# Where the activations of a feed-forward lie in SBUF, relative to the weights they meet

## The chip, the cores and the metric

One core of a Trainium2 chip runs the whole program in one launch. The metric is the device time of that core in microseconds. Three timed runs of the kernel before gave 2049.34 us in the median (2047.26 to 2052.21).

## The reference

Two blocks of layers, each of depth 2, on a sequence of 256 rows with 1024 columns in float32. The first block is a feed-forward, a mixer with sparse and block attention, and a second feed-forward:

```python
def swiglu(x, w_gate, w_up, w_down):
    return (jax.nn.silu(x @ w_gate) * (x @ w_up)) @ w_down

for l in range(DEPTH):
    x = x + 0.5 * swiglu(rms_norm(x, norm_ffn1[l]), ...)
    x = x + hybrid_mixer(rms_norm(x, norm_mix[l]), ...)
    x = x + 0.5 * swiglu(rms_norm(x, norm_ffn2[l]), ...)
```

The second block has a mixer with three branches (a recurrence, a retention and a spatial gate) and a feed-forward whose hidden columns go through a short convolution. A feed-forward widens 1024 columns to 2816 and comes back. There are six of them: four plain ones and two with convolution.

## The kernel before

Each float32 operand of a large product is held as two parts, a high one (rounded to the type float32r) and a low one (the rest). A product of two operands is three products on TensorE, `matmul3` (lines 82 to 90): high by high on line 88, high by low on line 89, low by high on line 90. In each the first operand (`lhs`) is loaded into the array as weights and the second (`rhs`) streams through it. A trace row names the moving operand first and the weights second.

A feed-forward (`ffn_phase`) runs over 11 chunks of 256 hidden columns. In a chunk, `hidden` makes the gate and up products: weights are 128 x 128 pieces of the gate and up matrices, the moving operand is the normed rows turned on their side, `hT`, 256 columns wide; that is 96 products. ScalarE and VectorE then form silu(gate) * up and split the outcome into a high and a low part in the tile `act`. In `down` the roles are turned: `act`, 128 x 128 at a time, is the weights, and the down matrix, 512 columns at a time, streams; that is 24 products a chunk. PE's order is hidden(i+1), down(i), hidden(i+2), down(i+1) and so on, so that a chunk's activations are ready long before they are used. Weights arrive by DMA in an `arrived` tile and are split by ScalarE (high, lines 384 and 394) and VectorE (low, lines 490 and 536) into `parts`.

Where the tiles lie is written out by hand, in columns of 4 bytes from a base. The plain feed-forwards use the map of the first block (`first_map`, base 45568), those with convolution the map of the second (`second_map`, base 58112). The start of a tile is base + 4 x column. Taken modulo 512 bytes:

| tile | plain feed-forwards | with convolution |
|---|---|---|
| `hT` (moving in gate and up) | 128 | 128 |
| gate and up parts (weights) | 448 | 448 |
| `act` (weights in down) | 128 | 128 |
| down parts (moving in down) | 448 | 448 |
| `arrived_down` (landing place) | 128 | 64 |

Other products of the same form lie elsewhere: the mixer's output product and its values job (`token_job`, projections by rows) have weights at 128 (`mixer_T_parts`) and a moving operand at 448 (`mixer_parts`); the second mixer's output product has weights at 320 (`merged_parts`) and a moving operand at 64 (`mix_parts`); its branch products have weights at 64 (`mix_parts`) and a moving operand at 64 (`branches_T`). Within these tiles the steps between slots, halves and parts are multiples of 512 bytes, but for the low part in the third slot of `mixer_parts`.

The distance between high and low part is 4096 bytes in `act` and `mix_parts`, 8192 in the down parts and in `merged_parts`.

Of the kernel before, what the change touches and what calls it, by code (L numbers as in the profile page):

```python
# [271 lines left out]
def blocks(first, *shape):  # L272

    width = KT * FF_W
    if not shape:
        return first
    step = width * int(np.prod(shape[1:]))
    return [blocks(first + n * step, *shape[1:]) for n in range(shape[0])]
# [526 lines left out]
def first_map(nc, c):  # L805

    def at(name, col, shape, dtype=F32):
        return nc.alloc_sbuf_tensor_at(name, shape, dtype, offset=FIRST_BASE + 4 * col)

    c.ffn = FfnMemory(at, "ffn", dict(hT=32, act=4128, arrived_down=6176, arrived=(blocks(9200, 2), blocks(23152, 2)),  # L810
                                      parts=(blocks(13296, 2, 2), blocks(27248, 2, 2)), down_parts=blocks(35440, 2, 2)))
    c.hT_parts = at("mixer_T_parts", 32, [P, 2, KT, S], F32R)
    c.wc1 = at("w_cmp1", 4128, [P, 2, CJ, CMP_HID])
    c.attention = at("attention", 4128, [P, 10 * S + N_WORK])
    c.branch_rows = at("branch_rows", 4128 + 10 * S + N_WORK, [P, 3, Q_COLS])
    c.wc2 = at("w_cmp2", 12320, [P, 2, 2, 2, DH])
    c.pos = at("pos", 43632 + W_UNIT, [P, 2, CJ])
    c.raw = at("raw", 12832, [P, N_TURNED, S])
    c.rot = at("rot", 17440, [P, N_ROT, S])
    c.vtok = at("v_tokens", 21024, [P, NT, 2 * P + Q_COLS])  # L820
    c.gates = at("gates", 22560, [P, NT, GATE_COLS])
    c.kc = at("k_cmp", 22608, [P, GROUPS, 16])
    c.vc = at("v_cmp_by_head", 22640, [P, NH, DH])
    widths = (UNIT, UNIT, W_UNIT)
    c.units_arrived = [at(f"mixer_arrived{n}", col, [P, w]) for n, (col, w) in enumerate(zip((23152, 25200, 43632), widths))]
    c.units_parts = [[at(f"mixer_parts{n}_{lo}", col + lo * w, [P, w], F32R)[:] for lo in range(2)] for n, (col, w) in enumerate(zip((27248, 31344, 35440), widths))]
    c.cos_part = c.work[:, 0:2 * S].rearrange("p (a n) -> p a n", a=2)

    c.kcols = c.h[:].rearrange("p t d -> p (t d)")[:, 0:2 * GROUPS * CJ * N_CMP].rearrange(
        "p (v g j n) -> p v g j n", v=2, g=GROUPS, j=CJ)  # L830
    hid_w = 2 * 2 * GROUPS * 16
    c.hid = c.work[:, 2 * S:2 * S + hid_w].rearrange("p (v f g n) -> p v f g n", v=2, f=2, g=GROUPS)
    c.hid_v = c.work[:, 2 * S + hid_w:2 * S + hid_w + 2 * NH * 16].rearrange("p (f g r n) -> p f g r n", f=2, g=GROUPS, r=REP)
# [800 lines left out]
def first_block(nc, c, c2, a, start, tables2, out):  # L1634
# [8 lines left out]
    def follow(before, ph):  # L1643
        before.nxt, ph.prev = ph, before

    first_map(nc, c)
    ffn1 = ffn(0, "ffn1")
    ffn1.start = start
# [9 lines left out]
    follow(ffn3, nsa2)  # L1658
    follow(nsa2, ffn4)
    second_map(nc, c2)  # L1660
    halves = [HalfUnits(c2, c2.half_sems, l) for l in range(DEPTH)]

# [187 lines left out]
def second_map(nc, c):  # L1850

    def at(name, col, shape, dtype=F32):
        return nc.alloc_sbuf_tensor_at(name, shape, dtype, offset=SECOND_BASE + 4 * col)
# [28 lines left out]
                     for n, cols in enumerate(((24272, 26320), (38608, 34512), (30416, 32464)))]  # L1882
# [14 lines left out]
    c.half_parts = [at(f"mix_parts{n}", col, [P, 2, HALF_UNIT], F32R) for n, col in enumerate((30416, 32464, 24272))]  # L1897
    c.y_rw_parts = at("rw_T_parts", 7208, [P, 2, 4, S], F32R)
    c.merged_parts = at("merged_parts", LOCAL, [P, 2, KT, S], F32R)
    c.conv_ffn = FfnMemory(at, "conv_ffn", dict(hT=18656, act=30432, arrived=(blocks(8240, 2), blocks(26320, 2)), arrived_down=12368,  # L1900
                                                parts=(blocks(48, 2, 2), ((36656, 38704), (24240, 40752))),
                                                down_parts=((14512, 16560), (32560, 34608)), taps=22752))

# [1405 lines left out]
```

## Time and profile before

| | |
|---|---|
| timed runs, median (lowest to highest) | 2049.34 us (2047.26 to 2052.21) |
| profiled execution: its span, the one time the trace states for it | 2044.7 us |
| TensorE products busy | 2006.7 us, 98% of the span, 17608 products |
| weight loads busy | 1861.9 us, 91% |
| VectorE busy | 1351.8 us, 66% |
| ScalarE busy | 1013.8 us, 50% |
| mean granted TensorE clock | 0.998 of full |

The busy time of an engine is the time in which at least one of its instructions runs. Products overlap in the records, since the end of one is modelled, so the pace of a row of products is read from one start to the next. Starts in the timeline are in microseconds from the start of the span, to 0.01.

### The profile page before, as it was taken

The page shows a single profiled execution, that of the slowest core. Times are in us where ns is not written, and L with a number is a line of the kernel's source. Part 1 is how long each engine was busy: PE and PEld are TensorE (multiplying, and loading weights), DVE is VectorE, ACT ScalarE, POOL GpSimd, SP SyncE. Part 2 cuts the span into 40 slices and gives each one's busy share as a digit, 9 for nine tenths or more (in the row PEclk, how much of TensorE's full clock was granted, in tenths as well). Part 3 has the DMA queues.
Part 4 walks back from the last instruction along what each step waited for, and adds up shares of the span by engine and source line. Part 5 has one row for each costly group of instructions (what it writes and reads, how often), then busy time and mean ns, then how long its engine had stood idle before and what let it go on. Part 6 is the DMA issues. An engine that isn't in the chain of part 4 may idle for free. (4 is left out here: it accounts for less than half of the span.)

```text
span 2044.7 us, 41739 instructions
## 1 busy us (share of the span) xinstructions
PE 2006.7 (98%) x17608; PEld 1861.9 (91%) x17608; DVE 1351.8 (66%) x2078; ACT 1013.8 (50%) x1462; POOL 12.9 (1%) x12
## 2 busy tenths in 40 slices
PE   8999999999999999999999999999999999999998
PEld 8999987999999998799989979989999988998997
DVE  6554776755655477575547766678776866578775
ACT  6333466533544346663336634465545644357443
POOL 0000000000000000000000010000000010000000
PEclk9999999999999999999999999999999999999999
DMA  7543732654464372364345324376544423357541
GB/s 307 195 196 114 255 115 84 251 201 155 185 246 187 116 246 89 124 238 185 144 168 196 119 85 145 110 252 248 185 155 155 139 108 122 123 178 271 193 185 52
DMA packets 79877, 348.79 MB, mean 171 GB/s; under 512 B 21232, under 2 KB 30576, under 8 KB 45808
## 3 DMA queue, kind: packets, MB, share of 16 engines
q1 hardware_dynamic: 79728, 346.61, 46.3%
q8 instruction: 117, 1.92, 0.4%
q14 instruction: 32, 0.26, 0.0%
HBM read 345.53 MB, written 1.05 MB: 169 GB/s over the span
## 5 line engine op out<-in xcount | busy, mean ns | idle before, releaser
L88 PE MATMUL bank<-ffn_hT_split,n_split_gate_up 128*128 128x256 f32 x1280 | 354.8, 277 | 0.0
L89 PE MATMUL bank<-ffn_hT_split,n_split_gate_up 128*128 128x256 f32 x1280 | 354.3, 277 | 0.0
L90 PE MATMUL bank<-ffn_hT_split,n_split_gate_up 128*128 128x256 f32 x1280 | 354.2, 277 | 0.0
L89 PEld LDWEIGHTS bank<-ffn_hT_split,n_split_gate_up 128*128 128x128 f32 x1280 | 240.5, 188 | 1.5
L88 PEld LDWEIGHTS bank<-ffn_hT_split,n_split_gate_up 128*128 128x128 f32 x1280 | 240.4, 188 | 1.5
L90 PEld LDWEIGHTS bank<-ffn_hT_split,n_split_gate_up 128*128 128x128 f32 x1280 | 240.4, 188 | 0.0
L413 ACT ACTIVATE work<-bank 128x256 f32<-128x256 f32 x88 | 32.8, 382 | 278.6 <-PE bank L90 274.2
L1939 DVE TENSOR_TENSOR mix_parts<-mix_arrived,mix_parts 128x1024 fp32r<-128x1024 f32 x88 | 107.5, 1223 | 88.8 <-ACT mix_parts L1934 88.6
L555 DVE TENSOR_TENSOR work<-bank,work 128x256 f32<-128x256 f32 x88 | 37.2, 423 | 177.6 <-ACT work L413 177.6
L536 DVE TENSOR_TENSOR ffn_split_down<-ffn_arrived_down,ffn_split_down 128x2048 fp32r<-128x2048 f32 x44 | 100.9, 2292 | 80.0 <-ACT ffn_split_down L394 80.0
L1934 ACT ACTIVATE mix_parts<-mix_arrived 128x1024 fp32r<-128x1024 f32 x88 | 92.9, 1057 | 105.2 <-PE bank L90 93.2
L490 DVE TENSOR_TENSOR n_split_gate_up<-arrived_gate_up,n_split_gate_up 128x2048 fp32r<-128x2048 f32 x60 | 135.9, 2287 | 11.6 <-ACT n_split_gate_up L384 11.6
L394 ACT ACTIVATE ffn_split_down<-ffn_arrived_down 128x2048 fp32r<-128x2048 f32 x44 | 84.8, 1927 | 110.9 <-PE bank L90 100.9
L90 PE MATMUL bank<-ffn_split_down,ffn_act_split 128*128 128x512 f32 x352 | 138.9, 394 | 0.0
L89 PE MATMUL bank<-ffn_split_down,ffn_act_split 128*128 128x512 f32 x352 | 138.0, 392 | 0.0
L88 PE MATMUL bank<-ffn_split_down,ffn_act_split 128*128 128x512 f32 x352 | 136.9, 389 | 0.0
L781 DVE TENSOR_TENSOR mixer_parts<-mixer_arrived,mixer_parts 128x512 fp32r<-128x512 f32 (+2 forms) x74 | 79.8, 1083 | 53.4 <-ACT mixer_parts L774 53.4
L384 ACT ACTIVATE n_split_gate_up<-arrived_gate_up 128x2048 fp32r<-128x2048 f32 x60 | 113.3, 1908 | 1.0 <-DMA arrived_gate_up<-in_ffn 0.9
L88 PE MATMUL bank<-normed_T_parts,mix_parts 128*128 128x256 f32 x384 | 110.0, 287 | 0.9 <-DVE mix_parts L1939 0.9
L89 PE MATMUL bank<-normed_T_parts,mix_parts 128*128 128x256 f32 x384 | 106.4, 277 | 0.0
L90 PE MATMUL bank<-normed_T_parts,mix_parts 128*128 128x256 f32 x384 | 106.4, 277 | 0.0
L536 DVE TENSOR_TENSOR conv_ffn_split_down<-onv_ffn_arrived_down,conv_ffn_split_down 128x2048 fp32r<-128x2048 f32 x22 | 50.4, 2292 | 63.4 <-ACT conv_ffn_split_down L394 63.3
(419 smaller groups left out, 5963.5 us busy)
## 6 DMA issues: line engine op xcount, KB each, us to landing
arrived_gate_up<-in_ffn SPq DMA_DIRECT2D x64, 1024.0 KB, 8.5
ffn_arrived_down<-in_ffn SPq DMA_DIRECT2D x44, 1024.0 KB, 4.8
mix_arrived<-in_mix_w SPq DMA_DIRECT2D x88, 512.0 KB, 3.6
rrived_gate_up<-in_conv_ffn SPq DMA_DIRECT2D x32, 1024.0 KB, 6.8
_arrived_gate_up<-in_ffn SPq DMA_DIRECT2D x24, 1024.0 KB, 6.7
mixer_arrived<-in_w_in SPq DMA_DIRECT2D x22, 1024.0 KB, 6.9
onv_ffn_arrived_down<-in_conv_ffn SPq DMA_DIRECT2D x22, 1024.0 KB, 4.8
irst_project_arrived<-in_w_in SPq DMA_DIRECT2D x17, 1024.0 KB, 4.9
```

The costliest lines, as they stand in the source:

```text
L88: pe.matmul(out, lhs[0], rhs[0], start=start, stop=False)
L89: pe.matmul(out, lhs[0], rhs[1], start=False, stop=False)
L90: return pe.matmul(out, lhs[1], rhs[0], start=False, stop=stop)
L384: act.activation(flat(w[part][slot][0]), arrived(part, slot), ACT.Copy).then_inc(s["gu_high"], 1)
L394: act.activation(flat(w[2][slot][0]), arrived(2, slot), ACT.Copy).then_inc(s["down_high"], 1)
L413: act.activation(acts[:, slot, f], c.ps[2 * slot + f][:, 0:S], ACT.Silu).then_inc(s["silu_ready"], 1)
L490: dve.tensor_tensor(flat(low), arrived(part, slot), plain(flat(high)), ALU.subtract).then_inc(s["gu_split"], 1)
L536: dve.tensor_tensor(flat(low), arrived(2, slot), plain(flat(high)), ALU.subtract).then_inc(s["down_split"], 1)
L555: dve.tensor_tensor(value, up, value, ALU.mult).then_inc(s["product_ready"], 1)
L781: last = eng.tensor_tensor(self.parts[slot][1][:, cols], self.arrived[slot][:, cols], plain(self.parts[slot][0][:, cols]), ALU.subtract)
L1934: act.activation(self.parts[n % RING][:, 0], self.arrived[n % RING], ACT.Copy).then_inc(self.s["half_high"], 1)
L1939: dve.tensor_tensor(low, self.arrived[n % RING], plain(high), ALU.subtract).then_inc(self.s["half_split"], 1)
```

## The change

`act` moves up by 16 columns, 64 bytes, in both maps. In the first map the landing place of the down weights, which followed it, moves by as much. Nothing else changes: modulo 512 bytes `act` is at 192 where it was at 128, and `arrived_down` of the plain feed-forwards at 192 where it was at 128.

```diff
-    c.ffn = FfnMemory(at, "ffn", dict(hT=32, act=4128, arrived_down=6176, arrived=(blocks(9200, 2), blocks(23152, 2)),
+    c.ffn = FfnMemory(at, "ffn", dict(hT=32, act=4144, arrived_down=6192, arrived=(blocks(9200, 2), blocks(23152, 2)),
...
-    c.conv_ffn = FfnMemory(at, "conv_ffn", dict(hT=18656, act=30432, arrived=(blocks(8240, 2), blocks(26320, 2)), arrived_down=12368,
+    c.conv_ffn = FfnMemory(at, "conv_ffn", dict(hT=18656, act=30448, arrived=(blocks(8240, 2), blocks(26320, 2)), arrived_down=12368,
```

## Rows read from the trace of the kernel before

**Rows 1.** The page, busy us by engine; granted clock in slices.
```profile
PE 2006.7 (98%) x17608; PEld 1861.9 (91%) x17608; DVE 1351.8 (66%) x2078; ACT 1013.8 (50%) x1462; POOL 12.9 (1%) x12
...
PEclk9999999999999999999999999999999999999999
```

**Rows 2.** Stretches, first and last of six feed-forward loops: length, busy, clock, DMA.
```profile
31.90:198.90 167.00, 167.00 (x1204) 156.18 (x1203) 93.75 (x102) 65.61 (x60) 0.20 (x1) 1.00 0.49 192
...
1868.80:2035.70 166.90, 166.90 (x1202) 155.78 (x1200) 123.64 (x184) 84.06 (x101) 0.00 (x0) 1.00 0.46 168
```

**Rows 3.** Groups by shape, one line of three of each kind of down product.
```profile
L88 PE MATMUL bank<-ffn_split_down,ffn_act_split 128*128 128x512 f32 x352 | 136.9, 389 | 0.0
...
L88 PE MATMUL bank<-conv_ffn_split_down,conv_ffn_act_split 128*128 128x512 f32 x176 | 68.5, 389 | 0.0
```

**Rows 4.** Timeline (start, length), PE, a down block and its follower.
```profile
73.02 0.39 PE L88 MATMUL bank<-ffn_split_down,ffn_act_split 128*128 128x512 f32 x1
...
78.28 0.39 PE L90 MATMUL bank<-ffn_split_down,ffn_act_split 128*128 128x512 f32 x1
78.51 0.28 PE L88 MATMUL bank<-ffn_hT_split,n_split_gate_up 128*128 128x256 f32 x1
```

**Rows 5.** Timeline, PE, 256-column products: gate and up twice, values job twice, branches.
```profile
28.77 0.28 PE L88 MATMUL bank<-ffn_hT_split,n_split_gate_up 128*128 128x256 f32 x1
...
31.25 0.28 PE L88 MATMUL bank<-ffn_hT_split,n_split_gate_up 128*128 128x256 f32 x1
...
63.16 0.28 PE L88 MATMUL bank<-ffn_hT_split,n_split_gate_up 128*128 128x256 f32 x1
...
65.88 0.28 PE L88 MATMUL bank<-ffn_hT_split,n_split_gate_up 128*128 128x256 f32 x1
...
298.64 0.28 PE L88 MATMUL bank<-mixer_parts,mixer_T_parts 128*128 128x256 f32 x1
...
299.32 0.28 PE L88 MATMUL bank<-mixer_parts,mixer_T_parts 128*128 128x256 f32 x1
...
816.45 0.28 PE L89 MATMUL bank<-mixer_parts,mixer_T_parts 128*128 128x256 f32 x1
...
817.51 0.28 PE L89 MATMUL bank<-mixer_parts,mixer_T_parts 128*128 128x256 f32 x1
...
1221.41 0.28 PE L88 MATMUL bank<-branches_T,mix_parts 128*128 128x256 f32 x1
...
1222.49 0.28 PE L88 MATMUL bank<-branches_T,mix_parts 128*128 128x256 f32 x1
```

**Rows 6.** Timeline, PE, the first mixer's output product, 12 products apart.
```profile
344.84 0.40 PE L88 MATMUL bank<-mixer_parts,mixer_T_parts 128*128 128x512 f32 x1
...
347.59 0.39 PE L88 MATMUL bank<-mixer_parts,mixer_T_parts 128*128 128x512 f32 x1
```

**Rows 7.** Timeline, PE, the second mixer's output: first, fourth and 28th product.
```profile
1341.23 0.39 PE L88 MATMUL bank<-mix_parts,merged_parts 128*128 128x512 f32 x1
...
1341.92 0.39 PE L88 MATMUL bank<-mix_parts,merged_parts 128*128 128x512 f32 x1
...
1347.36 0.39 PE L88 MATMUL bank<-mix_parts,merged_parts 128*128 128x512 f32 x1
```

**Rows 8.** Timeline, PE, first and seventh gate product behind a down block.
```profile
62.11 0.28 PE L88 MATMUL bank<-ffn_hT_split,n_split_gate_up 128*128 128x256 f32 x1
...
62.82 0.28 PE L88 MATMUL bank<-ffn_hT_split,n_split_gate_up 128*128 128x256 f32 x1
```

**Rows 9.** Groups by shape, DVE's subtractions for the down weights.
```profile
L536 DVE TENSOR_TENSOR ffn_split_down<-ffn_arrived_down,ffn_split_down 128x2048 fp32r<-128x2048 f32 x44 | 100.9, 2292 | 80.0 <-ACT ffn_split_down L394 80.0
L536 DVE TENSOR_TENSOR conv_ffn_split_down<-onv_ffn_arrived_down,conv_ffn_split_down 128x2048 fp32r<-128x2048 f32 x22 | 50.4, 2292 | 63.4 <-ACT conv_ffn_split_down L394 63.3
```

**Rows 10.** Timeline, DVE, the splits ahead of the block of rows 4.
```profile
58.02 0.43 DVE L559 TENSOR_TENSOR ffn_act_split<-work,ffn_act_split 128x256 fp32r<-128x256 f32 x1
...
61.26 2.29 DVE L490 TENSOR_TENSOR n_split_gate_up<-arrived_gate_up,n_split_gate_up 128x2048 fp32r<-128x2048 f32 x1
```

## The prediction

> **What bounds the kernel.** I began with the page's busy times: PE is busy for 98% of the span, its weight loads for 91% of it beside the products, and the granted clock stands at full in every slice [rows 1]. So the reader is to see a kernel in which a product that starts sooner moves everything behind it. The next view is the busy time in stretches, cut to the six feed-forward loops: PE's busy time equals each stretch to 0.01 us, in the first loop and in the last, at clock 1.00 [rows 2], while DVE is idle for 26 to 44% of it and ACT for half or more. These loops hold no wait of PE at all, only products back to back. The groups by shape say how many products the change touches: 352 on each of three lines in the four plain feed-forwards and 176 on each in the two with convolution [rows 3]. That is 3 × 528 = 1584 down products, 24 in each of 66 blocks (six feed-forwards of 11 chunks).
>
> The durations of those rows don't serve as prices, for a product's end is modelled and overlaps its follower. What counts is the distance from start to start, so the view that I lean on is the timeline. In one block of down products the first starts at 73.02 and the first product behind the block at 78.51: 5.49 us for 24, or 228.75 ns each [rows 4].
>
> **Why placement may be a price at all.** A product streams its moving operand while the weights of the next one are read. From the columns of the memory maps I work out the distance (start of the weights less start of the moving operand, in bytes modulo 512; the strides inside the tiles used here are multiples of 512, but for the low part in one slot of the mixer's ring, so one distance holds for a whole group). Down products now: 128 − 448 = 192. Gate and up: 448 − 128 = 320, which is 192 the other way round. The trace holds other distances as well. With 256 columns: the branch products at 0 take 1.08 us for 9, 120.0 ns each. At 192 and 320 there are two paces for the very same operands: the gate and up products take 2.72 for 24, 113.3, in the loops, but 2.48 for 21, 118.1, in the block at 28.77; the mixer's values job at 192 takes 0.68 for 6, 113.3, in one layer and 1.06 for 9, 117.8, in the other [rows 5]. Same shape, same clock: so distance sets which paces are open, and the way in chooses between them. With 512 columns the mixer's output product, also at 192 but in other tiles, takes 2.75 for 12, 229.2 each [rows 6], as the down products do. The output product of the second block's mixer stands at 320 − 64 = 256, the distance that the change makes and the farthest there is from 0: 5.44 us for 24, 226.67 each [rows 7]. That is exactly twice 113.3, so I read 226.67 as the pace with nothing lost to placement, and 192 as a loss of 228.75 − 226.67 = 2.1 ns a product.
>
> **The change part by part.** No instruction, wait or transfer is added or removed; three tiles move by 64 bytes.
>
> 1. The activations move from 128 to 192 modulo 512 in both maps, the down weights stay at 448: distance 256. If a down block goes at the pace of rows 7, it takes 5.44 instead of 5.49: 66 × 0.05 = 3.3 us. The merged product doesn't start at that pace: its first three take 0.69 against 0.68 [rows 7], 0.01 more. Down blocks are entered 60 times (the last two chunks of each feed-forward run as one), so with that run-in 0.6 us comes off: 2.7 us. The blocks of today show no such run-in, yet the merged product is the only row at 256; I take the middle, 3.0 us.
>
> 2. The seams. While the last up product streams the normed rows (at 128), the first activations are loaded: distance 0 today, 64 afterwards. While the last down product streams (at 448) the gate weights (at 448) are loaded: 0 before and after. One product per seam, at most 6.7 ns by the extremes of rows 5, either way: 60 × 6.7 = 0.4 us, kept for the range. Behind a down block the first six gate products take 0.71 us where six at pace take 0.68 [rows 8]: they enter at the slow pace and drop to the fast one, a run-in of 0.03 us. What makes them drop I can't read from the trace. I leave the seam as it is and make its two other ends rivals.
>
> 3. In the plain feed-forwards the landing place of the down weights moves too, from 128 to 192 modulo 512. The feed-forward with convolution keeps its own, at 64. From 128 and from 64 the subtraction that reads it takes 2292 ns [rows 9], so I put another 64 bytes at nothing; neither it nor the transfer is on PE's path.
>
> 4. Who is late next when PE runs 0.05 us a block faster? DVE's last subtraction for a chunk's activations ends at 58.02 + 0.43 = 58.45, and the down block that uses them begins at 73.02; the weights split from 61.26 to 63.55 are used at 78.51 [rows 4, 10]. The loop hands over with some 15 us in hand, so a shortening of 0.05 us in 16.4 finds no new wait, and the gain of every block goes through to the end.
>
> Sum: 3.0 us off the profiled execution's 2044.7 us, its span (the only time that the trace states for it). The median of the timed runs is 2049.3, 4.6 us more, which I take as lying around the span and untouched: 2049.3 − 3.0 = 2046.3 us.
>
> **The rivals.** *The run-in goes as well.* If the six slow products behind each of the 54 single down blocks come from the uneven pace at 192, that goes too: 3.3 + 54 × 0.03 = 4.9 us, 2044.4. For it: both paces are open at 320, and an even down block may lead straight into the fast one. Against it: the distance 0 at that seam stays. 10%.
>
> *Slower: the gate and up products stay in their slow pace.* The same seam, the other way: what leads them down to 113.3 after five products could be the phase in which today's down block ends, and behind an even one they would stay at 118.1, as they do in the block at 28.77. Price: 96 × (118.1 − 113.3) = 0.46 us a block, 54 blocks, 24.9 us, less the 3.0: 2071.2. It decides from one block in eight on (7 × 0.46 = 3.2). For it: two paces at one distance in rows 5, chosen by the way in. Against it: behind the loops' down blocks the drop comes at the same product every time, and the loops are long trains of products with no wait in them [rows 2], where the slow blocks of rows 5 follow other work. 12%.
>
> *The change doesn't do what it says.* The loss could belong to something that down products and mixer output share besides the distance, so that 256 changes nothing: 2049.3. For it: rows 7 are the only ones at 256, in a stage with other neighbours and with other steps between high and low parts (8192 bytes for the weights and 4096 for the moving operand, in the feed-forwards 4096 and 8192). Against it: rows 4 and 6 agree at 192 over two maps and different strides. 16%, with the halfway cases. The Trainium skill speaks for this rival: SBUF — State Buffer, section "Who interferes with whom", gives TensorE two independent read ports, one for the moving operand and one for weights, and says that it never waits on anyone; by that rule placement is free and the time stays at 2049.3. The trace does not agree: products of one shape at 113.3 and at 120.0 ns.
>
> **How the numbers follow.** Forecast 57%, run-in gone 10%, no change 16%, slow gate products 12%, something not listed 5%. The timed runs of before lie between 2047.3 and 2052.2, so about 0.2%, 4.1 us, is what a measurement here can tell from no change, and the forecast of 3.0 lies under it: measured, it comes out beyond 4.1 in perhaps four of ten. Faster by over 0.2%: 0.57 × 0.4 + 0.10 × 0.8, and a little from the rest, 33%. Slower: the slow gate products and some scatter, 13%. Within 0.2%: 54%. The range goes from the run-in case less the scatter of a median, 2042.5, to no change with a little scatter, 2050.5; the slower case is left out above.
>
> **What would show it.** Right: the starts in a down block lie 226 to 227 ns apart and a block takes 5.44 to 5.45 us instead of 5.49, in all six loops alike, with the gate and up products as before, PE still busy throughout and the span some 3 us shorter. The first products on each side of a block tell the run-ins. Wrong: blocks still at 5.49 (placement isn't the price), gate and up products at 118 ns beyond the sixth (the slower rival), or blocks at 5.44 and a span that doesn't follow (a wait that I don't see, which would stand in the loops' PE busy time).

## The result, and the profile after

The kernel became slower: 2065.19 us in the median of six runs (2063.05 to 2073.49) against 2048.27 for the kernel before (2044.30 to 2052.21), ratio 1.0092 [1.0077, 1.0107]. The forecast was 2046.3 with a range to 2050.5. The profiled execution has a span of 2063.9 us against 2044.7.

The page of the changed kernel, PE's busy time, the granted clock by slices, and two groups of products (line, operands, shapes, count, busy us, mean ns of one):

```profile
PE 2024.4 (98%) x17608; PEld 1882.0 (91%) x17608; DVE 1351.2 (65%) x2078; ACT 1013.3 (49%) x1462; POOL 12.9 (1%) x12
...
PEclk9999999999999999999999999999999999999999
...
L88 PE MATMUL bank<-ffn_hT_split,n_split_gate_up 128*128 128x256 f32 x1280 | 359.5, 281 | 0.0
...
L88 PE MATMUL bank<-ffn_split_down,ffn_act_split 128*128 128x512 f32 x352 | 137.0, 389 | 0.0
```

The first of these two groups in the kernel before:

```profile
L88 PE MATMUL bank<-ffn_hT_split,n_split_gate_up 128*128 128x256 f32 x1280 | 354.8, 277 | 0.0
```

The count of products is the same, the clock stands at 9 tenths or more in every slice as in [rows 1] (its mean is 0.999), and PE is still busy for 98% of the span: its busy time grew by 17.7 of the 19.2 us, so most of the loss is in the products, not in waits. The group that the change doesn't touch, gate and up products, has gone from a mean of 277 ns to 281; the group that it does touch shows 389 as before [rows 3]. The means hide what happened to the latter, because a product's modelled end overlaps its follower. The stretches show it: one down block and the gate block behind it, in the changed kernel (stretch in us, its length, PE's busy time and products, granted clock, DMA share, GB/s; the count takes in neighbours that reach into the stretch):

```profile
57.11:62.55 5.44, 5.44 (x26) 1.00 0.63 265
62.55:73.85 11.30, 11.30 (x97) 1.00 0.51 190
```

The down block takes 5.44 us, 226.7 ns a product, where [rows 4] had 5.49. The gate block takes 11.30 where the same block of the kernel before takes 10.91 (62.11 in [rows 8] to 73.02 in [rows 4]). The timeline shows the shape of it; its rows answer to those of [rows 5, 8] (start us, length of one):

```profile
62.55 0.28 PE L88 MATMUL bank<-ffn_hT_split,n_split_gate_up 128*128 128x256 f32 x1
...
63.26 0.28 PE L88 MATMUL bank<-ffn_hT_split,n_split_gate_up 128*128 128x256 f32 x1
...
66.08 0.28 PE L88 MATMUL bank<-ffn_hT_split,n_split_gate_up 128*128 128x256 f32 x1
```

The first six products take 0.71 us, as before. But the next 24 take 2.82 us, 117.5 ns each, where 24 of such a block take 2.72 in [rows 5], 113.3. The drop behind the fifth product does not come, in this block or in any of the 54 gate blocks that follow a single down block: by their starts, all take 11.306 or 11.307 us, against 10.905 to 10.907 before.

Summed from start to start over the trace, the growth of the span (19.15 us) is: gate and up products +21.94, down products −3.21, everything else +0.42. Of the 21.94, the 54 blocks at 0.40 each are 21.6; another 0.3 is the first gate block of one feed-forward, entered from the transposes, which went slow too (8.56 us for 72 products, where the other five keep 8.26). The plain feed-forwards and those with convolution slow down alike, though only in the plain ones did the landing place of the down weights move: the landing place is not the cause.

### The profile page after: what moved, and what is told of

Read it like the earlier page. It is cut to its first block and busy times, and to the rows that moved or that the text cites. A ratio compares the mean times of both kernels' runs of the same rounds, so it can differ in the third digit from the quotient of the medians.

```text
span 2063.9 us, 41739 instructions
## 1 busy us (share of the span) xinstructions
PE 2024.4 (98%) x17608; PEld 1882.0 (91%) x17608; DVE 1351.2 (65%) x2078; ACT 1013.3 (49%) x1462; POOL 12.9 (1%) x12
## 5 line engine op out<-in xcount | busy, mean ns | idle before, releaser
L88 PE MATMUL bank<-ffn_hT_split,n_split_gate_up 128*128 128x256 f32 x1280 | 359.5, 281 | 0.0
L89 PE MATMUL bank<-ffn_hT_split,n_split_gate_up 128*128 128x256 f32 x1280 | 359.2, 281 | 0.0
L90 PE MATMUL bank<-ffn_hT_split,n_split_gate_up 128*128 128x256 f32 x1280 | 359.1, 281 | 0.0
L384 ACT ACTIVATE n_split_gate_up<-arrived_gate_up 128x2048 fp32r<-128x2048 f32 x60 | 113.3, 1910 | 0.9 <-DMA arrived_gate_up<-in_ffn 0.7
```

Of the source, the lines that this page charges most:

```text
L88: pe.matmul(out, lhs[0], rhs[0], start=start, stop=False)
L89: pe.matmul(out, lhs[0], rhs[1], start=False, stop=False)
L90: return pe.matmul(out, lhs[1], rhs[0], start=False, stop=stop)
L384: act.activation(flat(w[part][slot][0]), arrived(part, slot), ACT.Copy).then_inc(s["gu_high"], 1)
```

## The experiments

Distances are, as ahead, weights less moving operand, modulo 512 bytes. "Gate block" is the 96 gate and up products behind a single down block, "down block" is 24 products; their times are distances between starts in the trace, and a step is one of each: 16.400 us in the kernel before, 16.747 in the changed one. Each run was one execution, with the kernel before on the same chip at 2044.1 us (runs 1 to 4), 2044.9 (5 to 8), 2046.5 (9 to 12) and 2051.0 (13 to 15). The effects looked for are 0.4 us a block, repeated in 18 or 36 blocks of one trace. A seam is the place where one block ends and the next begins, a train is a row of products without waits, and the slots 0 and 1 are the two sets of buffers that chunks use in turn. My theory was at first that at 320 two paces are open and the way into the block chooses between them, while at 256 only the fast one is; the rival was that the new place of the activations itself slows the gate products, whatever comes first.

**1. Gate and up products at 256 too (convolution only).** From the changed kernel:

```diff
-    c.conv_ffn = FfnMemory(at, "conv_ffn", dict(hT=18656, act=30448, ...
+    c.conv_ffn = FfnMemory(at, "conv_ffn", dict(hT=18672, act=30448, ...
...
-                                                ..., taps=22752))
+                                                ..., taps=22768))
```

> The changed kernel, with the normed rows (and the taps behind them) of the two feed-forwards with convolution moved by 64 bytes, so that their gate and up products stand at a distance of 256 instead of 320; the four plain feed-forwards stay as changed. Theory (at 192 and 320 two paces are open and the way in chooses; at 256 only the fast one): gate and up blocks with convolution take 10.88 us instead of 11.31, the plain ones stay at 11.31; span 2063.9 - 18 x 0.43 - 0.3 = about 2056. Rival (what slows the gate and up products is the new place of the activations itself, by the engines that write or read them there): both kinds stay at 11.31, span about 2064.

2073.3 us, span 2071.4. Its stretches, a down block and a gate block with convolution:

```profile
1405.83:1411.30 5.47, 5.47 (x27) 1.00 0.54 198
1411.30:1422.81 11.51, 11.51 (x97) 1.00 0.75 274
```

A miss: theory and rival both had less. The gate block is slower still: 11.51 / 96 = 119.9 ns, the pace that the branch products have at 0 [rows 5]. So 256 is no better than 0 for products of 256 columns, and "farthest from 0 is best", on which the forecast's reading of [rows 7] rested, is wrong as a general rule.

**2 and 3. One more product at every seam**, between the down block and the gate block: a small one of 128 columns in the plain feed-forwards, the first gate product twice with convolution. Run 2 adds it to the changed kernel, run 3 to the kernel before.

```diff
                     high, low = w[part][slot]
+                    if not after_first and f == 0 and part == 0:
+                        if conv is None:
+                            pe.matmul(bank[:, 0:P], c.ident, c.ident, start=True, stop=True)
+                        else:
+                            pe.matmul(bank[:, 0:S], high[:, 0, 0:P], hT[0][:, 0, :], start=True, stop=True)
```

> The changed kernel with one more product between each down block and the gate products behind it: in the plain feed-forwards a 128-column product of the identity with itself into a bank that is overwritten next, with convolution the first gate product a second time. Theory (the way in chooses the pace): at least one of the two kinds of seam lets its gate and up blocks return to some 10.9 us; if both do, span 2063.9 - 54 x 0.40 + 54 x 0.11 to 0.2 = 2048 to 2053; if only the plain ones, 2063.9 - 36 x 0.40 + 54 x 0.11 to 0.2 = 2055 to 2060. Rival (the place of the activations slows the products whatever comes first): all blocks stay at 11.31, span 2070 to 2075.

> The kernel before with the same two extra products at the seams. Theory (the way in chooses): the blocks take some 10.9 us or 11.31, all blocks of a kind alike; if the extra product leads into the fast pace by itself, span 2044.7 + 54 x 0.11 to 0.2 = 2051 to 2056; a kind that turns slow adds 0.40 a block, 14 us for the plain, 7 us for those with convolution, and would show that the old place of the activations doesn't protect. Rival (the place of the activations): no block slow, 2051 to 2056.

Spans 2072.4 and 2051.1. (The trace shows the small product as two records.) Gate blocks of the changed kernel with the extra product, plain and with convolution (the latter stretch holds the extra one):

```profile
61.93:73.32 11.39, 11.39 (x99) 1.00 0.52 196
...
1431.81:1443.24 11.43, 11.43 (x99) 1.00 0.45 164
```

and of the kernel before with it:

```profile
46.06:57.04 10.98, 10.98 (x99) 1.00 0.89 354
1417.96:1428.98 11.02, 11.02 (x99) 1.00 0.48 184
```

The slow blocks stay slow and the quick blocks quick, in all 54 of each: 11.39 − 10.98 = 0.41 is the whole difference again. Neither of these two extra products at the seam changes the outcome. By what was expected this is a point for the rival, the place of the activations; runs 4 to 6 and 13 answer it.

**4. Other distances for the down products**: 320 in the plain feed-forwards, 224 with convolution.

```diff
-    c.ffn = FfnMemory(at, "ffn", dict(hT=32, act=4144, arrived_down=6192, ...
+    c.ffn = FfnMemory(at, "ffn", dict(hT=32, act=4160, arrived_down=6208, ...
-    c.conv_ffn = FfnMemory(at, "conv_ffn", dict(hT=18656, act=30448, ...
+    c.conv_ffn = FfnMemory(at, "conv_ffn", dict(hT=18656, act=30440, ...
```

> The changed kernel with the activations at other distances from the down weights: 320 in the plain feed-forwards, 224 with convolution (gate and up products stay at 320). Theory: down products take 226.7 to 229 ns, even or in the uneven row of three; behind an even block the gate and up products stay slow (11.31 us), behind an uneven one they become fast (10.91), all blocks of a kind alike: a kind that is fast takes 14 us (plain) or 7 us (convolution) off the 2063.9. Rival (the place of the activations itself): gate and up blocks of some third length, not linked to the pace of the down block ahead of them.

Span 2070.1. Four consecutive blocks of a plain loop (down, gate, down, gate), then a pair with convolution:

```profile
73.46:79.05 5.59, 5.59 (x27) 1.00 0.51 214
79.05:90.36 11.31, 11.31 (x98) 1.00 0.50 187
90.36:95.96 5.60, 5.60 (x27) 1.00 0.45 187
95.96:106.86 10.90, 10.90 (x98) 1.00 0.48 180
1406.76:1412.36 5.60, 5.60 (x27) 1.00 0.69 237
1412.36:1423.67 11.31, 11.31 (x98) 1.00 0.77 281
```

This is the row that turned the explanation. All blocks of a kind were expected alike, yet at 320 gate blocks of 10.901 and 11.311 us alternate, in all four plain feed-forwards, with every operand in the same place modulo 512 each time. The down block behind a gate block of 10.901 takes 5.588 and leads into one of 11.311; the down block behind that takes 5.600 and leads back to 10.901. I read this as a state of the train of products, carried from block to block, which each down block here turns over. By itself this run doesn't show it, for the slots alternate too, and the slow gate blocks are those of slot 0 in all four feed-forwards. Run 5 separates the two, at 192. At 224 all 18 gate blocks stay slow (11.308) behind down blocks of 5.598, so a distance away from 256 is not enough to make them fast.

**5. The two slots apart** (plain: slot 0 at 256, slot 1 at 192 as before; convolution: activations at 256, gate and up at 192, the taps behind `hT` moving along, as in run 6).

```diff
-    c.ffn = FfnMemory(at, "ffn", dict(hT=32, act=4144, arrived_down=6192, ...
+    c.ffn = FfnMemory(at, "ffn", dict(hT=32, act=(4144, 5280), arrived_down=6320, ...
...
+        if isinstance(place["act"], tuple):
+            self.act = [at(f"{name}_act_split{slot}", col, [P, 2, 2, S], F32R) for slot, col in enumerate(place["act"])]
...
-    c.conv_ffn = FfnMemory(at, "conv_ffn", dict(hT=18656, act=30448, ...
+    c.conv_ffn = FfnMemory(at, "conv_ffn", dict(hT=18688, act=30448, ...
```

> From the changed kernel. Plain feed-forwards: the activations of slot 0 stay at distance 256, those of slot 1 lie at 192 as in the kernel before, so the down blocks alternate. Theory one (a down block alone decides how the gate and up products behind it go): blocks behind a down block at 256 take 11.307 us, blocks behind one at 192 take 10.906; the mean of the 36 blocks is 11.107, some 7 us less than the changed kernel in these four feed-forwards. Theory two (a down block at 192 hands on the pace that it was entered in): after the first block at 256 all are slow, 11.307. In both, down blocks at 256 take 5.440 and at 192 5.494. Feed-forwards with convolution: activations at 256, the normed rows 128 bytes further, so that gate and up products stand at 192 in place of 320. If only the distance without its sign counts, nothing changes there: 11.307 and 5.440. If the sign counts at that seam, the gate block is fast, 10.906.

Span 2065.4. Plain: a down block at 192 and its gate block, then one at 256 and its gate block; convolution, gate products at 192:

```profile
56.79:62.31 5.52, 5.52 (x27) 1.00 0.51 214
62.31:73.61 11.30, 11.30 (x97) 1.00 0.49 189
73.61:79.05 5.44, 5.44 (x26) 1.00 0.45 188
79.05:90.36 11.31, 11.31 (x97) 1.00 0.49 189
...
1426.12:1437.43 11.31, 11.31 (x98) 1.00 0.45 164
```

Theory two holds: entered behind a slow gate block, a down block at 192 does not lead back to the fast pace. It takes 5.513, not 5.494, and hands the slow pace on. The slot is not the cause: down and gate products of slot 1 lie, modulo 512, where they lie in the kernel before, and there the gate block is fast. What differs is the train ahead. So the kernel before was fast not because 192 makes gate products fast, but because its trains, entered fast once, stay so at 192. At 256 the first down block, entered from a gate block at the fast pace (8.26 us for 72), already leads into the slow pace, and none leads back. Other distances do lead back: in run 7 one feed-forward with convolution begins with a slow gate block (8.567 for 72), and the first down block at 384 leads to 10.889.

**6. PE empty at the seam** (plain only), from the changed kernel; convolution: gate and up products at 384.

```diff
         def hidden(i, slot, after_first=None):
+            if not after_first and conv is None:
+                pe.wait_ge(s["down_done"], n0["down_done"] + i - 1)
...
-    c.conv_ffn = FfnMemory(at, "conv_ffn", dict(hT=18656, act=30448, ...
+    c.conv_ffn = FfnMemory(at, "conv_ffn", dict(hT=18640, act=30448, ...
```

> From the changed kernel. Plain feed-forwards: PE waits, before the gate products behind a single down block, for that block's own last product, so that it runs empty there. Theory (the pace is set by the phase in which products follow products over the seam): entered from rest the block goes as the 72-product blocks behind the transposes do, 113.3 ns after the third product, 10.9 us and the wait itself, which I put at 0.1 to 0.3 us. Rival (the placement of the activations slows the gate products themselves, whatever the seam): 117.8 ns to the end, 11.3 us and the wait. Feed-forwards with convolution: the normed rows lie 64 bytes earlier, gate and up products at distance 384 with activations at 256. The 256-column products at 0 and 256 both take 120.0, so 384 should be like 128, which no run has shown yet: between 113.3 and 120.0 ns, 10.88 to 11.52 us a block.

Span 2077.7. Two plain gate blocks of the same feed-forward, then a pair with convolution:

```profile
45.27:56.27 11.00, 11.00 (x96) 1.00 0.88 354
62.03:73.44 11.41, 11.41 (x96) 1.00 0.52 199
1428.82:1434.31 5.49, 5.49 (x27) 1.00 0.75 264
1434.31:1445.82 11.51, 11.51 (x97) 1.00 0.40 149
```

Neither expectation as it stood: 13 of the 36 plain gate blocks are fast, 23 slow, with the same products at the same places modulo 512. Placement of the activations alone therefore doesn't slow gate products; the entry chooses. The first interval tells the two apart here without exception: 219 to 220 ns in the 23 slow blocks, 221 to 224 in the 13 others. Nor is it chance: the first, eighth and ninth block of each feed-forward, which stand outside PE's program loop, are fast in all four, and of the 24 inside the loop 23 are slow. Fast and slow blocks occur in both slots. A wait is no cure; rest does not lead to one pace. At 384 gate products take 119.9 ns, as at 0 and 256.

**7 and 8. More distances for the down products**: 128 plain and 384 with convolution (run 7); 0 plain and 128 with convolution (run 8).

Run 7:

```diff
-    c.ffn = FfnMemory(at, "ffn", dict(hT=32, act=4144, arrived_down=6192, ...
+    c.ffn = FfnMemory(at, "ffn", dict(hT=32, act=4240, arrived_down=6288, ...
-    c.conv_ffn = FfnMemory(at, "conv_ffn", dict(hT=18656, act=30448, ...
+    c.conv_ffn = FfnMemory(at, "conv_ffn", dict(hT=18656, act=30480, ...
```

Run 8:

```diff
-    c.ffn = FfnMemory(at, "ffn", dict(hT=32, act=4144, arrived_down=6192, ...
+    c.ffn = FfnMemory(at, "ffn", dict(hT=32, act=4208, arrived_down=6256, ...
-    c.conv_ffn = FfnMemory(at, "conv_ffn", dict(hT=18656, act=30448, ...
+    c.conv_ffn = FfnMemory(at, "conv_ffn", dict(hT=18656, act=30416, ...
```

> From the changed kernel, only the distance of the down products: 128 in the plain feed-forwards, 384 in those with convolution. Down products: measured so far are 228.9 ns at 192, 226.7 at 256, 233.3 at 224 and 320; if closeness to 0 costs, both lie between 226.7 and 240, twice the 120.0 of a 256-column product at 0, so 5.44 to 5.76 us a block. Gate blocks: if the length of the down block sets the phase of what follows, a block is 10.906 or 11.307, either one in every loop of a feed-forward or alternating as at 320; if only 192 leads into the fast pace, all are 11.307.

> From the changed kernel, only the distance of the down products: 0 in the plain feed-forwards, 128 in those with convolution. At 0 the 512-column products should be slowest: 240 ns, 5.76 us a block, if they behave as two 256-column ones at 0 do (120.0 each); if the row at 256 (226.7) and the row at 0 differ by nothing but the sign of half a period, 226.7. At 128 as in the plain feed-forwards of the run beside it. Gate blocks: 10.906 or 11.307 by the phase, as there; a fast one behind a down block of 5.44 would beat both kernels.

Spans 2049.1 and 2061.0. Run 7, plain at 128:

```profile
55.89:61.47 5.58, 5.58 (x27) 1.00 0.60 251
61.47:72.36 10.89, 10.89 (x98) 1.00 0.47 178
```

Run 8, plain at 0:

```profile
56.73:62.17 5.44, 5.44 (x27) 1.00 0.54 226
62.17:73.48 11.31, 11.31 (x98) 1.00 0.49 187
```

A clear miss at 0, where I had put the slowest down products: 0 gives the same two blocks as 256 to the nanosecond (5.440, 11.307), and 384 the same as 128 (5.577, 10.890). For down products the pattern repeats in 256 bytes. So what is best for 512 columns (0 and 256: 226.7 ns, twice 113.3) is, with 384, the worst for 256 columns (119.9 to 120.0). Behind down blocks at 128 every single gate block is fast, though the down products are slower there than at 192.

**9 and 10. A few products at another distance.** The low part of the activations, weights of every third down product, is moved away from 256: in run 9 only that of a chunk's second half (four products, the last one among them), in run 10 all of it (eight). Plain to 128, convolution to 192.

In run 9 `act` becomes two tiles, and its users ask for a piece by part, slot and half (tiles at columns 4144 and 5776, 30960 and 30432):

```diff
-        self.act = at(f"{name}_act_split", place["act"], [P, 2, 2, 2, S], F32R)
+        kind, first, second = place["act"]
...
+            most = at(f"{name}_act_split0", first, [P, 2, 3, S], F32R)
+            rest = at(f"{name}_act_split1", second, [P, 2, S], F32R)
+            self.act = lambda lo, slot, f: rest[:, slot] if lo and f else most[:, slot, 2 * lo + f]
```

In run 10 the tiles are the high and the low part (columns 4144 and 5264, 31472 and 30432):

```diff
+            tiles = [at(f"{name}_act_split{lo}", col, [P, 2, 2, S], F32R) for lo, col in enumerate((first, second))]
+            self.act = lambda lo, slot, f: tiles[lo][:, slot, f]
```

> From the changed kernel: of each chunk's activations only the low part of the second half lies elsewhere. It is the weights of every sixth... of four down products of a block, the third of each group of three in the block's second half, the last product of the block among them. Plain feed-forwards: those four at distance 128, the other twenty at 256; with convolution: the four at 192. Theory one (the last products before the seam decide): gate blocks go as behind blocks wholly at 128, 10.890 us, in the plain ones; with convolution fast, 10.906, or slow as they came. Theory two (the state is that of the whole train; one product can't turn it, as the extra product of the second experiment could not): 11.307 in both. Down blocks if each product keeps the pace of its own distance: 20 x 226.7 + 4 x 232.4 = 5.463 in the plain ones, 20 x 226.7 + 4 x 228.9 = 5.449 with convolution. If theory one holds in the plain ones, block and gate block together are 16.353 against 16.400 in the kernel before, and this version is a little faster than both.

> From the changed kernel: all low parts of the activations (the weights of each third down product) lie at distance 128 in the plain feed-forwards and at 192 in those with convolution; the high parts stay at 256. Theory one (the last product decides): gate blocks 10.890 in the plain ones. Theory two (the share of products at 256 decides): 11.307 still. Down blocks if each product keeps the pace of its distance: 16 x 226.7 + 8 x 232.4 = 5.486 and 16 x 226.7 + 8 x 228.9 = 5.458. A block shorter or longer than that would show that the pace of a product depends on its neighbours too.

Spans 2066.1 and 2061.7. Run 9, plain:

```profile
56.43:61.92 5.49, 5.49 (x26) 1.00 0.60 239
61.92:73.23 11.31, 11.31 (x98) 1.00 0.49 188
```

Run 10, plain, then with convolution:

```profile
57.37:62.91 5.54, 5.54 (x26) 1.00 0.49 209
62.91:74.22 11.31, 11.31 (x98) 1.00 0.50 193
1423.91:1429.46 5.55, 5.55 (x27) 1.00 0.55 199
1429.46:1440.36 10.90, 10.90 (x98) 1.00 0.51 189
```

Neither theory holds as put. The last product does not decide (run 9: slow in all 54). Nor can the share alone be the rule: eight products at 128 leave the gate blocks slow, eight at 192 make them fast. The seam ahead of the down block doesn't decide either: in run 10 the first weights of each down block, a high part, lie as in the changed kernel, and with convolution the gate blocks are fast all the same. The block times miss the sum of single paces: 5.493 against 5.463 and 5.449 expected in run 9, 5.547 and 5.550 against 5.486 and 5.458 in run 10. So a product's pace is not given by its own two addresses alone; a train of mixed distances costs more than the sum of its parts.

**11 and 12. The remaining places**: down products at 160 plain and 352 with convolution (run 11); at 288 plain, and with convolution gate and up products at 224 (run 12).

Run 11:

```diff
-    c.ffn = FfnMemory(at, "ffn", dict(hT=32, act=4144, arrived_down=6192, ...
+    c.ffn = FfnMemory(at, "ffn", dict(hT=32, act=4248, arrived_down=6296, ...
-    c.conv_ffn = FfnMemory(at, "conv_ffn", dict(hT=18656, act=30448, ...
+    c.conv_ffn = FfnMemory(at, "conv_ffn", dict(hT=18656, act=30472, ...
```

Run 12:

```diff
-    c.ffn = FfnMemory(at, "ffn", dict(hT=32, act=4144, arrived_down=6192, ...
+    c.ffn = FfnMemory(at, "ffn", dict(hT=32, act=4152, arrived_down=6200, ...
-    c.conv_ffn = FfnMemory(at, "conv_ffn", dict(hT=18656, act=30448, ...
+    c.conv_ffn = FfnMemory(at, "conv_ffn", dict(hT=18680, act=30448, ...
...
-                                                ..., taps=22752))
+                                                ..., taps=22776))
```

> From the changed kernel, only the distance of the down products: 160 in the plain feed-forwards, 352 in those with convolution. So far 0 and 256 agree to 0.001 us a block (5.440, gate blocks 11.307), and so do 128 and 384 (5.577, 10.890): distances count modulo 256. By that, 160 and 352 (like 96) are new. Between their neighbours 128 (232.4 ns) and 192 (228.9 to 229.7), 160 should take some 231 ns, 5.53 us a block, with gate blocks fast; 96 between 64 (233.3) and 128 some 233 ns, 5.59 us, gate blocks either. Rival: no order in the distances at all.

> From the changed kernel. Plain feed-forwards: down products at 288, like 32 by the period of 256: between 256 (226.7) and 320 (233.3), some 230 ns, 5.52 us a block; gate blocks slow, 11.307, since both sides of 256 (192 entered slow, 224) kept them slow. With convolution: activations stay at 256, the normed rows lie 96 bytes further, gate and up products at 224. Measured for 256 columns are 192 and 320 (113.3 or 117.8), 160 and 384 (119.7 to 120.0), 256 (120.0); 224 should lie between 192 and 256: 118 to 120 ns, 11.3 to 11.5 us. If it is below 11.3, the gate products have a better place behind an even down block.

Spans 2051.1 and 2057.6. Run 11, plain, then with convolution:

```profile
57.09:62.69 5.60, 5.60 (x27) 1.00 0.59 244
62.69:73.60 10.91, 10.91 (x98) 1.00 0.49 179
1427.16:1432.77 5.61, 5.61 (x27) 1.00 0.70 270
1432.77:1443.68 10.91, 10.91 (x97) 1.00 0.41 152
```

Run 12, plain, then with convolution:

```profile
57.33:62.93 5.60, 5.60 (x27) 1.00 0.55 233
62.93:73.82 10.89, 10.89 (x98) 1.00 0.48 179
1431.35:1436.81 5.46, 5.46 (x26) 1.00 0.80 290
1436.81:1448.02 11.21, 11.21 (x98) 1.00 0.40 142
```

At 160, 288 and 352 the down products are as slow as at 320, and all gate blocks fast; at 288 I had expected slow. Gate products at 224 take 116.7 ns, the least of all places tried for them behind a down block at 256 (117.8 at 320).

**13. The kernel before, PE empty at the seam** (plain); the changed activations in the feed-forwards with convolution alone, which is half of the change by itself.

```diff
-    c.ffn = FfnMemory(at, "ffn", dict(hT=32, act=4144, arrived_down=6192, ...
+    c.ffn = FfnMemory(at, "ffn", dict(hT=32, act=4128, arrived_down=6176, ...
...
         def hidden(i, slot, after_first=None):
+            if not after_first and conv is None:
+                pe.wait_ge(s["down_done"], n0["down_done"] + i - 1)
```

> The kernel before in the plain feed-forwards (distance 192), but PE waits for the down block's last product ahead of each of their gate blocks, as in the drained run at 256. Theory (the entry alone chooses between the two paces of the gate products): blocks of both paces appear here too, 11.0 and 11.4 us with the entry, though without the wait all 36 go fast; the first interval tells which, 219 to 220 ns before a slow one and 221 to 224 before a fast one, as in the drained run. Rival (down products at 256 make the gate products slow): all 36 at 11.0. Feed-forwards with convolution: activations at 256, so the change stands there alone: gate blocks 11.307, down blocks 5.440.

Span 2072.9. A plain gate block, and a down block with convolution:

```profile
46.34:57.75 11.41, 11.41 (x96) 1.00 0.87 328
1428.82:1434.26 5.44, 5.44 (x27) 1.00 0.58 221
```

The theory's main point holds, against the rival: with down products at 192, where all 36 gate blocks are fast without the wait, 14 of 36 now go slow. The 219 to 224 rule of run 6 doesn't carry over: slow blocks begin with 217 (one), 219 (five), 221 (three) and 222 (five), the others with 217, 218, 223 and 224. The place in the program tells more here too: the first, second and eighth block are slow in all four feed-forwards, the ninth is fast, and of the 20 between, 18 are fast. With convolution the change alone gives 5.440 and 11.307, as in the whole change: the two kinds of feed-forward do not act on each other.

**14 and 15. Another place for the gate products behind a down block at 256**: convolution, activations at 256, gate and up at 288 (run 14) and 352 (run 15); plain as in the kernel before.

Run 14 (run 15 is the same with `hT=18648` and `taps=22744`):

```diff
-    c.ffn = FfnMemory(at, "ffn", dict(hT=32, act=4144, arrived_down=6192, ...
+    c.ffn = FfnMemory(at, "ffn", dict(hT=32, act=4128, arrived_down=6176, ...
-    c.conv_ffn = FfnMemory(at, "conv_ffn", dict(hT=18656, act=30448, ...
+    c.conv_ffn = FfnMemory(at, "conv_ffn", dict(hT=18664, act=30448, ...
...
-                                                ..., taps=22752))
+                                                ..., taps=22760))
```

> Plain feed-forwards as in the kernel before: gate blocks 10.906, down blocks 5.494. Feed-forwards with convolution: activations at 256, gate and up products at 288. Measured for 256 columns: 117.8 (or 113.3) at 320, 120.0 at 256; in between 118 to 120 ns, 11.3 to 11.5 us, and nothing gained. If there is a fast pace at 288 that an even down block leads into, 10.9 us, this beats the kernel before by 18 x 0.05 = 1 us.

> Plain feed-forwards as in the kernel before: 10.906 and 5.494. Feed-forwards with convolution: activations at 256, gate and up products at 352: between 320 (117.8 or 113.3) and 384 (119.9), 113 to 120 ns; at 224, the mirror place by the period of 256 being 288, it was 116.7. Fast behind an even block would be 10.9 us and 1 us gained on the kernel before.

Spans 2058.9 and 2054.6. Run 14, a plain gate block, then a pair with convolution:

```profile
61.95:72.86 10.91, 10.91 (x98) 1.00 0.47 180
1425.49:1430.98 5.49, 5.49 (x27) 1.00 0.80 309
1430.98:1442.34 11.36, 11.36 (x98) 1.00 0.36 130
```

Run 15, a pair with convolution:

```profile
1424.46:1429.93 5.47, 5.47 (x27) 1.00 0.84 307
1429.93:1441.32 11.39, 11.39 (x97) 1.00 0.34 131
```

Both about 118.5 ns a gate product: no place tried lets a down block at 256 be followed by a fast gate block. The plain feed-forwards, put back, are fast again (10.906 in all 36).

All distances of the down products, with gate and up at 320, by starts in the traces:

| distance | modulo 256 | down block, us | gate block behind it | step |
|---|---|---|---|---|
| 0, 256 (changed) | 0 | 5.440 | 11.307 | 16.747 |
| 288 | 32 | 5.593 | 10.893 | 16.487 |
| 320 | 64 | 5.588 / 5.600 | 11.311 / 10.901 | 16.700 (mean) |
| 352 | 96 | 5.611 | 10.916 | 16.527 |
| 128, 384 | 128 | 5.577 | 10.890 | 16.467 |
| 160 | 160 | 5.597 | 10.910 | 16.507 |
| 192 (before) | 192 | 5.494 | 10.906 | 16.400 |
| 192 behind a slow gate block | 192 | 5.513 | 11.307 | 16.820 |
| 224 | 224 | 5.598 | 11.308 | 16.907 |

None of the fifteen beats the kernel before; its step is the shortest of all. The shortest down block with the shortest gate block would be 5.440 + 10.890 = 16.330, and no run shows the two together.

## Why the prediction was wrong

Step 1, the down products, was right: blocks of 5.440 us (the first of a feed-forward 5.455, one 5.485, so the run-in of [rows 7] appears there alone), −3.2 us in all against the −3.0 that I took and the 3.3 without a run-in. The "change does nothing" rival didn't happen: placement moved the down products and the gate products both, in opposite directions. The Trainium skill (SBUF — State Buffer, "Who interferes with whom") gives TensorE independent read ports for the two operands; the conclusion that placement is therefore free does not agree with these traces, where a down block went from 5.494 to 5.440 us and a gate block from 10.906 to 11.307.

Step 2 failed: "What makes them drop I can't read from the trace. I leave the seam as it is". The term that it so put at nothing, beside the 0.4 us kept for the range, came to +21.6 us: each of 54 gate blocks went from 10.906 to 11.307. The slower rival happened, with its mechanism as it was put (the state in which the down block ends decides) and nearly its size: 54 × 0.40 where it said 54 × 0.46. The price was a little high for two reasons of 0.03 us each: the gate blocks of the kernel before are not fast throughout (their slow head is in the 10.906), and the 118.1 ns, read off 21 products, is 117.8 over a whole block.

Two arguments against that rival were weak, and the runs show why. "The drop comes at the same product every time" was taken as a sign of robustness. But 54 equal hand-overs are one observation repeated 54 times; change it and all 54 go the other way together, as they did. And "the slow blocks follow other work" explained the wrong thing away: [rows 5] showed one product with two paces, chosen by the way in, and a change to the products just ahead is a change of the way in. With no means to tell which way the hand-over would fall, 12% for a loss seven times the expected gain was too little; among the six other places modulo 256 tried, it fell slow in one, fast in four, and alternated in one.

The premise behind step 1 was also wrong, though its number came out: [rows 7] were read as "256 is farthest from 0, so nothing is lost". The number didn't need it, for [rows 7] were themselves taken at 256. Runs 1 and 8 show that 0 and 256 give the same pace, the best for 512 columns and (with 384) the worst for 256. Steps 3 and 4 held: the feed-forwards with and without a moved landing place slowed alike, and PE's busy time fills the blocks shown as before. (One reading of [rows 2] was a shade off: in the last loop ScalarE is idle for 49.6% of the time, not for half or more. Nothing hangs on it.)

What stays open is the rule by which a down block hands over one state or the other. That there are two paces for the same operands, that the one entered lasts through blocks, and that it is chosen at entry, is shown (runs 5, 6 and 13, with run 4 agreeing). Why the place in the program goes with the outcome in runs 6 and 13 was not looked into. That the state is a phase between the reading of the streaming operand and that of the next weights is only argued.

## What to carry to other kernels

In a train of products without waits, the pace of one block can hang on how the block ahead of it ends, so a cheaper block must be priced together with what follows it. If a trace shows one product at two paces with the same operands, treat any edit upstream of it as able to choose between them, and price the whole train at the slower one as a rival. Placement of two operands is worth a scan: with gate and up products at 320, steps here lie between 16.40 and 16.91 us for nothing but a tile's start.

## What the runs showed of the hardware that I had not expected

- For the down products the distance between weights and moving operand counts modulo 256 bytes: 0 and 256, and 128 and 384, agree within 1 ns a block (runs 7 and 8). Only the weights moved in these runs; that it is the distance, and not their own address, rests on [rows 7], where 226.67 ns were measured at 256 with both operands elsewhere.
- The steady loops run in whole multiples of 6.667 ns, which is 16 cycles at 2.4 GHz, the level of the granted clock. One step is 16.400 us = 2460.0 of them in the kernel before, 16.747 = 2512.0 in the changed one, 16.467 = 2470.0 at 128, 16.487 = 2473.0 at 288, 16.507 = 2476.0 at 160, 16.527 = 2479.0 at 352; two steps at 320 are 33.400 = 5010.0. The single paces fit too: 113.33 is 17, 120.0 is 18, 226.67 is 34, and 117.8 is 53 for three products. The blocks by themselves (10.906, 5.494) are no such multiples; only their sum is. Why it is so stays open.
- An entry from an empty PE is no reset: in the drained runs it led to the slow pace in 23 of 36 blocks and in 14 of 36; within a run these are nearly the same blocks of all four feed-forwards.
